# A decoder trunk in one kernel: six of eleven feature groups of each FFN down projection by one level of Strassen's scheme

## The reference

```python
def swiglu(x, w_gate, w_up, w_down):
    return (jax.nn.silu(x @ w_gate) * (x @ w_up)) @ w_down
# x (512, 1024), w_gate and w_up (1024, 2816), w_down (2816, 1024)
```

## Time and profile before

| | |
|---|---|
| median of 3 runs | 2355.29 us (2354.16 to 2356.46) |
| the profiled execution | 2354.63 us |
| its span, first to last instruction | 2352.9 us |
| PE busy | 2331.8 us, 99% of the span |
| DVE busy | 1151.1 us, 49% |
| ACT busy | 881.6 us, 37% |
| POOL busy | 179.0 us, 8% |
| granted TensorE clock, mean | 0.997 |

### The profile page before, as it was taken

One profiled execution on the slowest core, in us unless ns is written; L12 is line 12 of the kernel. 1 busy time (PEld: TensorE's weight loads), 2 busy tenths in 40 slices (PEclk: granted clock), 3 DMA queues, 4 the chain that ended last, 5 costly groups with the idle time before them and its releaser, 6 DMA issues.

```text
span 2352.9 us, 30267 instructions
## 1 busy us (share of the span) xinstructions
PE 2331.8 (99%) x12035; PEld 1976.7 (84%) x12035; DVE 1151.1 (49%) x1531; ACT 881.6 (37%) x1442; POOL 179.0 (8%) x150
## 2 busy tenths in 40 slices
PE   8999999999999999999999999999999999999998
PEld 7888888888888888888888888888878888888887
DVE  4433436595645444433454433455996544443434
ACT  4322324444444443323333322335265443322322
POOL 0131100000000001100101000000000000100000
PEclk9999999999999999999999999999999999999999
DMA  5233332311222123233223332322322212332231
GB/s 183 81 108 98 92 114 76 104 63 58 79 83 97 63 72 111 86 107 99 94 95 99 98 99 90 107 90 90 108 72 84 88 54 90 99 108 94 85 107 72
DMA packets 170483, 217.48 MB, mean 92 GB/s; under 512 B 12952, under 2 KB 120824, under 8 KB 170360
## 3 DMA queue, kind: packets, MB, share of 16 engines
q1 hardware_dynamic: 170248, 215.75, 28.8%
q10 hardware_dynamic: 112, 0.03, 0.0%
HBM read 213.63 MB, written 2.10 MB: 92 GB/s over the span
## 4 chain that ended last, share of the span: by engine, by line
PE 98%; DVE 1%; ACT 1%; issue 0%; DMA 0%; ACTq 0%; POOLq 0%; POOL 0%; DVEq 0%
PE ps L1682 29%; PE ps L1683 29%; PE ps L1684 29%; PE ps L2120 1%; PE ps L2233 1%; PE ps L1764 1%; PE ps L2050 1%; PE ps L1866 1%; PE ps L2158 1%; PE ps L2064 0%; PE ps L1734 0%; PE ps L2209 0%; PE ps L2147 0%; PE ps L1718 0%; PE ps L2160 0%
## 5 line engine op out<-in xcount | busy, mean ns | idle before, releaser
L1682 PE MATMUL ps<-xlo,whi 128*128 128x512 f32 (+1 forms) x2032 | 752.1, 370 | 1.7 <-DVE wlo L1074 1.7
L1683 PE MATMUL ps<-xhi,wlo 128*128 128x512 f32 (+1 forms) x2032 | 748.9, 369 | 0.0
L1684 PE MATMUL ps<-xhi,whi 128*128 128x512 f32 (+1 forms) x2032 | 748.8, 368 | 0.0
L1074 DVE SCALAR_TENSOR_TENSOR wlo<-raw,vec,whi 128x512 fp32r<-128x512 f32 (+1 forms) x488 | 338.6, 741 | 412.4 <-ACT whi L642 411.1
L642 ACT ACTIVATE whi<-raw,vec 128x512 fp32r<-128x512 f32 (+1 forms) x488 | 318.6, 708 | 486.2 <-PE ps L1684 450.9
L1682 PEld LDWEIGHTS ps<-xlo,whi 128*128 128x128 f32 x2032 | 384.0, 189 | 65.7 <-issue 2.1
L1684 PEld LDWEIGHTS ps<-xhi,whi 128*128 128x128 f32 x2032 | 383.7, 189 | 63.9
L1683 PEld LDWEIGHTS ps<-xhi,wlo 128*128 128x128 f32 x2032 | 383.9, 189 | 63.1
L1069 DVE TENSOR_TENSOR wlo<-raw,whi 128x1024 fp32r<-128x1024 f32 x152 | 185.5, 1227 | 286.2 <-ACT whi L638 284.7
L638 ACT ACTIVATE whi<-raw 128x1024 fp32r<-128x1024 f32 x152 | 159.4, 1056 | 336.3 <-PE ps L1684 335.8
L1682 PE MATMUL ps<-wlo,mid_hi 128*128 128x512 f32 x704 | 274.4, 390 | 0.0
(11 more groups left out here) (248 smaller groups left out, 2213.4 us busy)
## 6 DMA issues: line engine op xcount, KB each, us to landing
raw<-ffn_w_gate_dram SPq DMA_DIRECT2D x176, 256.0 KB, 2.8
raw<-ffn_w_up_dram SPq DMA_DIRECT2D x176, 256.0 KB, 3.0
raw<-ffn_w_down_dram SPq DMA_DIRECT2D x176, 256.0 KB, 3.1
raw<-xattn_w_kv_dram SPq DMA_DIRECT2D x64, 256.0 KB, 3.0
raw<-even_w_in_dram SPq DMA_DIRECT2D x56, 256.0 KB, 2.9
raw<-odd_w_in_dram SPq DMA_DIRECT2D x42, 256.0 KB, 2.8
raw<-xattn_w_q_dram SPq DMA_DIRECT2D x32, 256.0 KB, 3.0
raw<-xattn_w_o_dram SPq DMA_DIRECT2D x32, 256.0 KB, 3.0
```

What stands on the lines that cost most here:

```text
L1074: last = v.scalar_tensor_tensor(out=lo[:, k, :], in0=full[:, k, :], scalar=vec[:, c:c + 1], in1=hi[:, k, :].bitcast(f32), op0=MUL, op1=SUB)
L1682: mm(out_ap, lh, rl, start=start, stop=False, skip_group_check=skip_group_check)
L1683: mm(out_ap, ll, rh, start=False, stop=False, skip_group_check=skip_group_check)
L1684: return mm(out_ap, lh, rh, start=False, stop=stop, skip_group_check=skip_group_check)
```

## The change

The hidden groups are now taken as `FF_GROUPS = ((0, 3), (3, 3), (6, 5))`. The first two passes of an FFN end in a stage `quads` in place of `down`, the third in a plain `down`. A quad is one group of 256 features: its activation is a 2x2 block matrix of feature tiles (odd, even) and token halves, its weights a 2x2 block matrix of the same feature tiles and column halves. One level of Strassen's scheme (in Winograd's form) takes seven block products in place of eight, for four sums of activation blocks (S1 to S4) and four of weight blocks (T1 to T4).

- SP loads three of the four weight corners of a pass (nine DMAs of 256 KB) into tensors `w11`, `w12` and `w21` of their own, by `load_corners`; the fourth corner comes through two pieces of `raw`.
- DVE makes the sums T1 to T4 in place, mostly in the last group of the gate and up stage, for the last quad within the `quads` stage. At the end of each group that will be a quad it makes S1 to S4; `mid_hi` and `mid_lo` get seven blocks of 128x256 where there were four, in two steps.
- A pass has 21 units of 128x512 of weights in 11 pieces (`quad_pieces`); each unit feeds two token tiles, 6 matmuls. The products accumulate over the three quads in PSUM and some of them onto each other, and DVE reads banks into `y_rows` ten times in a pass, in `reads_of`, between its splits. TensorE waits for these reads (`product_read`) before it starts S2, S4, S3 and A22 products.
- POOL's product is now in place in `mid` (silu(gate) times up), of the same size. `make_tables` moves to the stage `even_in`, and DVE's two operations on the tables move to just before its memset of `scoresT`. The loops of the gate and up stages are written out.

The diff, cut to what the text speaks of:

```diff
-FF_PASSES = ((0, 6), (6, 5))
+FF_GROUPS = ((0, 3), (3, 3), (6, 5))
+QUADS = 3
+def quad_units():
+    early, late = range(QUADS - 1), QUADS - 1
+    out = [(name, q) for name in ("T1", "B11", "B21") for q in early]
+    out += [("B11", late), ("B21", late), ("T1", late)]
+    return out + [(name, q) for name in ("T2", "B22", "T3", "T4") for q in range(QUADS)]
...
# SP
+        def load_corners(k, l, j):
+            base, _, q0 = passes[k]
+            w = A["ffn_w_down"][l, j]
+            if k:
+                sp.wait_ge(lo_made, passes[k - 1][0] + len(quad_pieces()) + RAW_SLOTS)
+            if k == 0:
+                sp.wait_ge(memT_ready, 1)
+            elif q0 == 0:
+                sp.wait_ge(pieces_used, base - 4 * FF_GROUPS[0][1] + 1 + SPLIT_SLOTS)
+            for t, loaded, odd, c0 in ((w11, w11_loaded, 1, 0), (w12, w12_loaded, 1, GC), (w21, w21_loaded, 0, 0)):
+                for q in range(QUADS):
+                    k0 = (2 * (q0 + q) + odd) * P
+                    sp.dma_start(t[:, q, :], w[k0:k0 + P, c0:c0 + GC]).then_inc(loaded, 16)
...
+                for g in range(ng):
+                    for kp in range(4):
...
+                        load(loads, gate_and_up(l, j, kp, (g0 + g) * 256))
+                        loads += 1
+                    if g == 0 and piece and piece + 4 * ng in pass_of:
+                        load_corners(pass_of[piece + 4 * ng], l, j)
+                    if g == ng - 1 and not piece:
+                        load_corners(0, l, j)
...
# DVE, end of a gate and up group that will be a quad
+                    v.tensor_tensor(paired(mid[:, 4:8, :]), PS[:, bank:bank + 2, :], rows_scale, MUL).then_inc(gate_scaled, 1)
+                    v.tensor_tensor(paired(mid[:, 0:4, :]), PS[:, bank + 2:bank + 4, :], rows_scale, MUL).then_inc(up_scaled, 1)
                     dve.wait_ge(up_scaled, mids).then_inc(bank_free[bank // 4], 1)
+                    if g == ng - 1 and not plain:
+                        split_next()
...
+                    dve.wait_ge(product_ready, mids)
+                    a12, a22, a11, a21 = [mid[:, 4 + n, :] for n in range(4)]
+                    E.run(v.tensor_tensor(mid[:, S1, :], a21, a22, ADD))
+                    first_sum = E.last
+                    E.run(v.tensor_tensor(mid[:, S3, :], a11, a21, SUB))
+                    dve.wait_ge(*first_sum)
+                    E.run(v.tensor_tensor(mid[:, S2, :], mid[:, S1, :], a11, SUB))
+                    E.own()
+                    v.tensor_tensor(mid[:, S4, :], a12, mid[:, S2, :], SUB).then_inc(sums_ready, 1)
+                    dve.wait_ge(mid_hi_ready, 2 * mids - 1)
+                    v.tensor_tensor(mid_lo[:, g, 4:7, :], mid[:, 4:7, :], mid_hi[:, g, 4:7, :].bitcast(f32),
                                     SUB).then_inc(mid_lo_ready, 1)
+                    if g == ng - 1:
+                        split_next()
+                    dve.wait_ge(mid_hi_ready, 2 * mids)
+                    v.tensor_tensor(mid_lo[:, g, 0:4, :], mid[:, 0:4, :], mid_hi[:, g, 0:4, :].bitcast(f32),
+                                    SUB).then_inc(mid_lo_ready, 1)
...
# DVE, stage quads
+            t2_sums(k, late, 1)
+            split_next()
+            read["P1"]()
+            split_next()
+            read["P2"]()
+            read["P5"]()
+            t3_sums(k, late, 1)
+            split_next()
+            t4_sums(k, late, 1)
+            split_next()
+            split_next()
+            read["P6"]()
+            split_next()
+            read["P3a"]()
+            read["P3b"]()
+            release()
+            split_next()
+            read["P7a"]()
+            read["P7b"]()
+            split_next()
+            read["P4a"]()
+            split_next()
+            read["P4b"]()
+            release()
...
# PE, stage quads; both_tiles is 6 matmuls, one_tile 9
+            for q in range(early):
+                both_tiles(q, S1, z, q == 0)
+            wait_banks(E.group + 1)
+            for q in range(early):
+                both_tiles(early + q, A11, x, q == 0)
+            for q in range(early):
+                both_tiles(2 * early + q, A12, y_bank, q == 0)
+            u0 = 3 * early
+            both_tiles(u0, A11, x, False, True)
+            both_tiles(u0 + 1, A12, y_bank, False, True)
+            both_tiles(u0 + 2, S1, z, False, True)
+            u0 += 3
+            pe.wait_ge(product_read, r0 + 1)
+            for t in range(2):
+                one_tile(u0, t, S2, x)
+            pe.wait_ge(product_read, r0 + 3)
+            for t in range(2):
+                one_tile(u0 + QUADS, t, S4, z)
+            pe.wait_ge(product_read, r0 + 4)
+            for t in range(2):
+                one_tile(u0 + 2 * QUADS, t, S3, x)
+            for t in range(2):
+                pe.wait_ge(product_read, r0 + 7 + t)
+                one_tile(u0 + 3 * QUADS, t, A22, x)
```

More of the change, by code:

```diff
@@ L64, with quad_pieces, piece_of @@
 N_VEC = CONV_TAPS + CONV_W * CONV_T
+def quad_units():
[3 more added lines that the diff above has]
+    return out + [(name, q) for name in ("T2", "B22", "T3", "T4") for q in range(QUADS)]
+def quad_pieces():
+    units = quad_units()
+    corners, sums = units[:3 * QUADS], units[3 * QUADS:]
+    return [part[n:n + 2] for part in (corners, sums) for n in range(0, len(part), 2)]
+def piece_of(unit):
+    return unit // 2 if unit < 3 * QUADS else (3 * QUADS + 1) // 2 + (unit - 3 * QUADS) // 2
 def stages():
@@ L461, in forget_rows @@
             return halves
-        piece = ended = 0
+        piece = ended = loads = 0
         for kind, l, arg, ng, np_ in STAGES:
@@ L506, in _ @@
                         src = two_rows(w, 2 * kp, g * GC)
-                    load(piece, 0, src)
+                    load(loads, src)
+                    loads += 1
                     piece += 1
@@ L587, in _ @@
             if kind == "gate_up":
[L588 to L600, removed]
+                for g_ in range(ng):
+                    products += 1
+                    pool.wait_ge(gate_silu, products)
+                    pool.wait_ge(up_scaled, products)
+                    g.tensor_tensor(mid[:, 4:8, :], mid[:, 4:8, :], mid[:, 0:4, :], MUL).then_inc(product_ready, 1)
+            elif kind == "even_in":
                 make_tables()
-            elif kind == "even_in":
                 power(16)
@@ L1452, in _ @@
                     continue
-                if kind == "down":
-                    E.group_done()
-                    for t in range(TT):
-                        E.run(v.tensor_copy(y_rows[:, t, columns(g)], PS[:, bank + t, :]), y_ready)
-                    E.release_banks()
-                elif name == "c_v":
+                if name == "c_v":
                     E.group_done()
@@ L2032, in _ @@
                     if kind == "down":
-                        pe.wait_ge(mid_lo_ready, m0 + kp + 1)
-                        last = token_major(slot, kp, n_kp, bank, mid_hi, mid_lo, range(TT))
+                        pe.wait_ge(mid_lo_ready, 2 * (m0 + kp + 1))
+                        last = token_major(slot, kp, n_kp, bank, plain_hi, plain_lo, range(TT))
                     else:
```

346 lines of the change are left out of this document (267 added, 79 removed).

## The result

The changed kernel takes **2379.97 us** (median of four runs, 2377.76 to 2383.3) against 2355.03 us for the kernel before beside it; the ratio is 1.0106, with a 95% interval of 1.0089 to 1.0124. It is slower by 25 us. The forecast was 2364 us with a range of 2340 to 2378: the sign was right, the size was not, and the result lies just outside the range. The profiled execution took 2379.67 us.

The account below looks back on a forecast made before the run. TensorE was taken as the bound; -32.6 us of matmuls, +24.8 for quad passes, +16.5 for corner loads and +0.5 for small edits gave +9.2 on 2354.6, so 2364 us, with an 80% range of 2340 to 2378.

Parts of the forecast that it names:

- What bounds the kernel: Whole kernel: TensorE, busy 2331.8 of 2352.9 us; a matmul removed or a wait added counts in full.
- The saving: Down projections: quads need 42 matmuls in place of 48, 144 fewer in all, saving 32.6 us.
- VectorE's queue in a quad pass: Quad passes: TensorE waits for VectorE's splits and reads, adding 3.1 us a pass, 24.8 us for eight.
- The walk: VectorE's queue stepped through one quad pass from the last gate and up matmul: 31.65 us against 28.56 of matmuls.
- Rival 1: Quad passes: GpSimd doesn't delay VectorE, so 1.9 us a pass and 2354 us, no change; chance 0.16.
- The corner loads: Head of group 1 in three FFNs: its loads queue behind nine corner DMAs, TensorE waits 5.5 us each, 16.5 us.
- My upper end of 8: Head of group 1: upper bound of 8 us each if the corners move at 318 GB/s.
- The landing: Group 1's first piece: released at 875.1, landing at 884.2 us, with 1.8 us fixed and 2.88 MB at 393 GB/s.
- The small edits: Gate and up stages, moved tables and unrolled loops: 0 to 2 us added, taken as 0.5.
- rival 2: Corner loads cost next to nothing, 1 us each: 2340 to 2350 us, middle 2346, faster; chance 0.16.
- rival 3: Nearly all the saving kept, under 1 us a quad pass and small load cost: 2335 us; chance 0.10.
- Rival 4: Waiting VectorE ops don't overlap, 5.5 us a quad pass, and loads cost 7 each: 2388 us; chance 0.10.

Follow-up runs that it names:

- the kernel with all four edits: Changed kernel with corner loads behind group 1's, row-scale copy before the split, last group's product on VectorE, and VectorE's quad-pass queue reordered: 2324.65 us, ratio 0.9866.

## Why the prediction was wrong in size, point by point

- **What bounds the kernel** was right: the table above closes with waits of TensorE and its slow clock alone, though VectorE is busy for 57% of the span only.
- **The saving**, 32.6 us, was right; the kernel with all four edits shows it.
- **VectorE's queue in a quad pass**, 3.1 us forecast, 3.11 to 3.35 measured. The walk's waits of 0.3, 0.6, 0.65, 0.75 and 0.65 us were 0.58, 0.49, 0.49, 0.68 and 0.66, and the first, 0.16, was 0.06. Single waits were off by up to 0.28 us upwards and 0.16 downwards, so it is in part luck that their sum came out within 0.1 to 0.3. The split that I started only behind GpSimd's product, at 5.15 on the clock of the walk, ended at 92.03 - 85.76 = 6.27; I had 6.4. The rule of the Trainium skill (SBUF — State Buffer, section "SBUF: two separate sides") holds here: 2.67 us beside the product, 1.28 clear of it. Rival 1, no blocking, is out.
- **The corner loads**, 5.5 us a head forecast, 9.67 to 10.71 measured. This is the term that was mis-sized, and it is nearly the whole miss: 30.1 - 16.5 = 13.6 of 25.0 - 9.2 = 15.8 us (the passes add 1.0, the rest 1.3). The mechanism, its three places and its releasers were as forecast (the last releaser was `rsb`, right behind the `wlo` that I named). My upper end of 8 fits the gaps alone, 7.64 to 8.43, and leaves no room for what follows them. Three things were missing from the 5.5; over the three heads they are 5.7, 2.0 and 5.9 us, together the 13.6.
  - *The landing.* I let 2.88 MB move at 393 GB/s, the best window of the trace, from the first microsecond on: 9.1 us after the release. It took 10.57, 11.04 and 11.35. The windows show 223 GB/s, then 293, before the rate reaches 378; in the other two FFNs the same two windows have 241 and 277, 214 and 284. (The first window holds some of the fixed 1.8 us, the second none.) A rate read in the middle of a long burst is not that of its first microseconds; why it starts lower, no run shows.
  - *The chain behind it.* From ScalarE's start to TensorE's I had 2.8 us and it took 3.48. The bank for the row scales came behind the late split; 0.4 of it, by the experiment that moved the copy.
  - *The clock.* 2.02, 1.61 and 2.28 us, 5.9 in all, at 0.50 after each wait. It stood nowhere in the sum. The earlier trace rows gave the price of a matmul at full clock, and I used it for a stretch behind an idle time that my own forecast made 5.5 us long. Shown by the run with the added matmuls: waits of 1.0 to 1.4 us are left, and no half clock.
- **The small edits**, forecast at 0.5 us, cost nothing that can be seen: the part of the even mixer in which the tables are now made and used (388.66 to 549.45 us before, 387.18 to 547.97 here) takes 160.79 us in both. The 1.8 us of the last row lie elsewhere. The even mixer is 1.4 us shorter, because its clock was at half for 6.8 us and not for 10.2 (windows of PE, the kernel before, then the changed one):

```profile
589.90:600.10 10.20, 10.20 (x40) 0.50 0.16 51
```

```profile
589.99:596.80 6.81, 6.66 (x23) 0.50 0.24 77
```

  The odd mixer is 3.2 us longer. It has 32 matmuls of one column each; in the kernel before they took 3.63 us, at full clock, and full clock followed. Here the clock fell to 0.50 within them, at 1822.2 us, and stayed there for 6.8 us (time line of PE):

```profile
1819.77 4.60 PE L1994 MATMUL ps<-ones,ring 128*128 128x1 f32 x32
1824.23 0.77 PE L1942 MATMUL ps<-wlo,xhi 128*128 128x512 f32 x1
1824.80 0.63 PE L1943 MATMUL ps<-whi,xlo 128*128 128x512 f32 x1
```

  Nothing of the change stands in either place. In the runs with the loads moved and with the added matmuls the odd mixer was 1.6 us longer than before, not 3.2. Why it differs between kernels stays open; no run was made for it. Between two of the kernels here these two mixers alone can make 3 to 4 us each.
- **Rivals 2 and 3** (loads free, saving kept) are out for this kernel. The kernel with the loads moved has the time of rival 2 (2346.92 against 2346) and the one with all four edits is faster than rival 3 (2324.65 against 2335), but both got there by an edit and not by the rivals' reasons. **Rival 4**, 2388, had the loads at 7 us a head, still too low, and the passes at 5.5, far too high.

## What to carry to other kernels

An edit that puts loads ahead of others in one queue is to be costed to the start of the work that waits: release, the slower rate at the start of the burst, landing, the work of ScalarE and VectorE on the piece, and the slow clock after the wait. In this case every gap of 3.9 to 9.0 us in TensorE's work brought 1.5 to 3.0 us more behind it, unless other matmuls filled the gap. Before giving up an algorithm whose saving is swallowed, look at which two or three waits swallow it: here moving one line in SyncE's order, giving one product to VectorE and reordering VectorE's queue (with the copy of the row scales moved too) turned 25 us slower into 31 us faster.

## What was unexpected of the hardware

- Behind 18 gaps of 3.9 to 9.0 us in its work, three in each of six kernels, TensorE's granted clock was 0.50, the 1.2 GHz level, for a matmul spacing of 0.427 us in place of 0.227, and the loss behind it, 1.5 to 3.0 us, wasn't smaller for the short gaps than for the long ones. The Trainium skill (TensorE: Matmul & The Clock Gate, "Part 1: The HAM clock gate") says that the clock is gated when the engine idles and is released by activity; the run with the added matmuls agrees, with 1.00 in place of 0.50.
- Nine DMAs of 256 KB, with others behind them, moved 214 to 241 GB/s in the first 3 us and 277 to 293 in the next, in the three heads of the changed kernel, and 378 to 385 only after that; a corner took 4.3 us from issue to landing where a pair's DMA took 3.1.
- A pair of 128x512 subtractions on VectorE took 2.67 us beside a GpSimd product and 1.28 without it, and GpSimd needs 2.41 us for a product that VectorE does in 1.23.
